# Second layer's stream: six pieces of weights multiplied by Strassen's seven products instead of plainly

## The reference, cut to what matters

```python
    for i in range(DEPTH):
        ...
        x, ctx = trunk_layer(x, ctx, c, c_ctx, p, ang_r, ang_c, need_ctx=(i < DEPTH - 1))
    return x
```

## Time and profile before

| what | value |
|---|---|
| runs | 1561.01, 1561.46, 1563.44 us, median 1561.46 us |
| the profiled execution's own time | 1564.0 us |
| its span (first to last instruction) | 1562.2 us |
| TensorE busy | 1516.4 us, 97% |
| VectorE, ScalarE, GpSimd busy | 681.1, 415.0, 281.9 us |
| mean granted TensorE clock | 0.995 |
| the second a layer begins (its first transposes) | 652.96 us after the start of the span |

### The profile page before, as it was taken

One profiled execution on the slowest core, in us unless ns is written; L12 is line 12 of the kernel. 1 busy time (PEld: TensorE's weight loads), 2 busy tenths in 40 slices (PEclk: granted clock), 3 DMA queues, 4 the chain that ended last, 5 costly groups with the idle time before them and its releaser, 6 DMA issues.

```text
span 1562.2 us, 19171 instructions
## 1 busy us (share of the span) xinstructions
PE 1516.4 (97%) x7888; PEld 1077.2 (69%) x7888; DVE 681.1 (44%) x1460; ACT 415.0 (27%) x814; POOL 281.9 (18%) x314
## 2 busy tenths in 40 slices
PE   6999999999999999999999999999999999999997
PEld 2544544455688885555877888588888758888873
DVE  1233433464633343523344311365687216568721
ACT  1122325232312210121235320134233213423320
POOL 0322210131455441113002102110100011010010
PEclk9999999999999999999999999999999999999999
DMA  8642222300122231322322243423221323332231
GB/s 362 262 175 108 108 108 108 135 27 17 65 81 81 97 123 68 150 108 97 119 108 108 102 156 120 175 102 144 109 110 71 147 115 149 126 112 106 88 128 40
DMA packets 17370, 184.22 MB, mean 118 GB/s; under 512 B 2306, under 2 KB 2818, under 8 KB 4740
## 3 DMA queue, kind: packets, MB, share of 16 engines
q1 hardware_dynamic: 17284, 183.01, 30.7%
HBM read 181.95 MB, written 1.05 MB: 117 GB/s over the span
## 4 chain that ended last, share of the span: by engine, by line
PE 89%; ACT 3%; DVE 3%; issue 2%; DMA 1%; POOL 1%; SPq 0%; POOLq 0%; ACTq 0%; DVEq 0%
PE ps L756 86%; PE ps L811 3%; DVE arena L1749 1%; DVE arena L1755 1%; DMA arena<-in_wf 1%; POOL arena L2362 1%; ACT arena L1333 1%; ACT L1709 0%; ACT L1707 0%; DVE arena L1752 0%; ACT arena L1577 0%; ACT arena L1707 0%; ACT arena L1593 0%; ACT L1595 0%; ACT L1593 0%
## 5 line engine op out<-in xcount | busy, mean ns | idle before, releaser
L756 PE MATMUL ps<-arena 128*128 128x256 f32 (+7 forms) x7396 | 1467.1, 383 | 33.8 <-DMA arena<-in_wf 12.3
L756 PEld LDWEIGHTS ps<-arena 128*128 128x128 f32 (+5 forms) x7396 | 1023.6, 178 | 445.4 <-issue 311.9
L2362 POOL TENSOR_TENSOR arena<-arena 128x256 f32<-128x256 f32 (+6 forms) x254 | 247.3, 994 | 825.8 <-DVE arena L1755 409.3
L1755 DVE SCALAR_TENSOR_TENSOR arena<-arena 128x256 f32<-128x256 f32 (+4 forms) x470 | 231.0, 545 | 143.4 <-ACT arena L1475 38.8
L1333 ACT ACTIVATE arena<-ps 128x512 f32<-128x512 f32 (+2 forms) x280 | 134.9, 505 | 448.3 <-PE ps L756 370.5
L1749 DVE TENSOR_TENSOR arena<-arena 128x512 f32<-128x512 f32 (+14 forms) x190 | 140.4, 761 | 170.9 <-ACT arena L1333 95.8
L1755 DVE SCALAR_TENSOR_TENSOR arena<-arena,ps 128x256 f32<-128x256 f32 (+2 forms) x121 | 54.0, 456 | 207.2 <-PE ps L756 96.9
L1749 DVE TENSOR_TENSOR arena<-ps,arena 128x512 f32<-128x512 f32 (+16 forms) x120 | 48.8, 434 | 106.0 <-PE ps L756 97.3
L811 PEld LDWEIGHTS ps<-arena 128*128 128x128 f32 x488 | 55.7, 141 | 29.4 <-issue 19.5
L811 PE MATMUL ps<-arena 128*128 128x128 f32 x488 | 71.5, 278 | 3.1 <-ACT arena L1611 1.5
L1752 DVE TENSOR_SCALAR arena<-arena 128x256 f32<-128x256 f32 (+9 forms) x181 | 62.8, 382 | 15.7 <-POOL arena L2362 10.8
(11 more groups left out here) (96 smaller groups left out, 294.4 us busy)
## 6 DMA issues: line engine op xcount, KB each, us to landing
arena<-in_wf SPq DMA_DIRECT2D x69, 2048.0 KB, 8.3
arena<-in_wf SPq DMA_DIRECT2D x22, 1024.0 KB, 6.5
arena<-in_wf SPq DMA_DIRECT2D x2, 1152.0 KB, 7.7
arena<-in_xinT SPq DMA_DIRECT2D x2, 1024.0 KB, 15.9
arena<-in_xin SPq DMA_DIRECT2D x4, 512.0 KB, 3.9
arena<-in_rp SPq DMA_DIRECT2D x2, 1024.0 KB, 8.2
arena<-in_consts SPq DMA_DIRECT2D x1, 1410.0 KB, 21.6
arena<-in_pa SPq DMA_DIRECT2D x2, 532.0 KB, 9.4
```

The costliest lines, as they stand in the source:

```text
L756: return e.matmul(o, l, r, start=start, stop=stop, skip_group_check=True)
L1755: return e.scalar_tensor_tensor(out=o, in0=x, scalar=s, in1=y, op0=op0, op1=op1)
L2362: return e.tensor_tensor(o, x, y, op)
```

## The change

Each of six pieces of weights of the second layer (`ag`, `gg`, `su`, `mg0`, `ms0`, `ma1`) is multiplied by seven products of a quarter size. The weights are cut in four quarters (512 input features x 256 output features), the inputs in four (512 features x 128 tokens). A product is eight matmuls of 128 x 128 weights with 128 x 128 inputs (two chunks of output features, four blocks of input features). The four steps of a piece stay where they are in the order and hold products 1 and 2, 6 and 7, 5 and 4, and 3.

- GpSimd makes four sums of weight quarters for each piece (`seven_weights`), two in the step before the piece (`w1`) and two in its first step (`w2`). Three of the four lie in `WW`, one in place of quarter 21 in the ring.
- VectorE makes four differences of the inputs once, ahead of `ag`'s first sum (`HW`).
- Products 6, 5 and 3 go on adding into the bank of product 1, after ScalarE has copied out what stood there; product 4 goes on in the bank of product 7. VectorE makes three sums for each piece (`seven_sums`). In the gated pieces tanh is made by quarters, four instead of four by chunks.
- `HW`, `WW` and a copy `EW` lie in units 4 to 6 of the ring. From `a1ag` to `a1ma1` the ring has four units, and a load waits for the piece two places ahead.

The core of the diff (`seven_result` gives the place of a quarter of the result; `rest_free` is the end of the pieces that lay in units 4 to 6):

```diff
+SEVEN = [[],
+         [("ag", "T"), ("gg", "T"), ("su", "A"), ("mg0", "G"), ("ms0", "G"), ("ma1", "G")]]
...
+    for name, kind in SEVEN[l]:
+        i = [s[:1] for s in steps].index([(name, 0, "T" if kind == "T" else "A")])
+        for k in range(4):
+            steps[i + k] = [(name, x[0], "W" + kind) for x in WINOGRAD[2 * k:2 * k + 2]]
+        steps[i - 1] = steps[i - 1] + [("w1", name, "-")]
+        steps[i] = steps[i] + [("w2", name, "-")]
...
+                if kind[0] != "W":
+                    hold(("dense", l, n, i), b, (dense_act if kind == "A" else dense_dve)(l, n, i))
+                    b = 1 - b
+                elif i == 1:
+                    hold(("dense", l, n, 1), b, dense_dve(l, n, "g12") if kind == "WT" else dense_act(l, n, 3))
+                elif i in (2, 7):
+                    hold(("dense", l, n, i), 1 - b, dense_dve(l, n, 2 if i == 2 else 4))
+                elif i == 3:
+                    b = 1 - b
...
+        short, units = ("a1ag", "a1ma1"), NU
         for name, w in PLAN:
             k = -(-w // UNIT)
-            at = at if at + k <= NU else 0
+            if name == short[0]:
+                rest_free = [done_with[x] for x in tenant[4:] if x]
+                tenant[4:], units = ["rest"] * 3, 4
+            at = at if at + k <= units else 0
...
+            def one_of_seven(l, n, x):
+
+                w = use(f"a{l}{n}", 8)
+                _, s, t, _ = WINOGRAD[[y[0] for y in WINOGRAD].index(x)]
+                if x in (1, 2, 7):
+                    b = bank("dense", l, n, x)
+                else:
+                    b = psum("dense", l, n, 7 if x == 4 else 1)
+                    p.wait_ge(dense_act(l, n, {6: 1, 5: 6, 4: 7, 3: 5}[x]))
...
+                if len(s) == 1:
+                    p.wait_ge(seven_sum(l, n, s))
+                if len(t) == 1:
+                    p.wait_ge(dense_dve(l, "hs", int(t) - 1))
...
+                m = 128 if l else 256
+                for c in range(2):
+                    for k in range(4):
+                        ins = mm(b[:, m * c:m * c + m], W[:, k, 128 * c:128 * c + 128], H[:, k],
+                                 x in (1, 2, 7) and c == k == 0, k == 3)
+                return ins
...
+                if x == 1:
+                    copy(seven_result(l, n, 1, 1), b, scale=scale).then_inc(event(1), 1)
+                elif x == 6:
+                    copy(seven_result(l, n, 2, 1), b).then_inc(event(6), 1)
+                elif x == 7:
...
+                    copy(two_chunks(l, EW), b).then_inc(event(7), 1)
+                    if kind != "WA":
+                        last_th = tanh(1, 1, seven_result(l, n, 1, 1), last_th)
+                elif x == 5:
+                    copy(seven_result(l, n, 2, 2), b).then_inc(event(5), 1)
+                elif kind == "WA":
+                    copy(seven_result(l, n, 1, 2), b, scale=scale).then_inc(event(3), 1)
+                else:
+                    last_th = tanh(2, 1, seven_result(l, n, 2, 1), last_th)
+                    last_th = tanh(1, 2, b, last_th)
...
+                if x in (2, 5, 4):
+                    f, t = {2: (1, 1), 5: (2, 2), 4: (2, 1)}[x]
+                    o = seven_result(l, n, f, t)
+                    b = two_chunks(l, EW if x == 5 else psum("dense", l, n, 7 if x == 4 else 2))
+                    v.wait_ge(dense_done(l, n, x), dense_act(l, n, {2: 1, 5: 5, 4: 6}[x]))
...
+                def make(s, x, y, op, product):
+
+                    if product:
+                        g.wait_ge(*([dense_done(l, SEVEN[l][k - 1][0], product)] if k else rest_free))
+                    tt(w21 if s == "1" else WW[s], x, y, op).then_inc(dn_w.hit(0, 4 * k + "3214".index(s)), 1)
+
+                if first:
+                    g.wait_ge(pieces[name][2])
+                    make("3", w11, w21, ALU.subtract, 7)
+                    g.wait_ge(seven_sum(l, n, "3"))
+                    make("2", w22, WW["3"], ALU.subtract, 6)
+                else:
+                    make("1", w21, w22, ALU.add, None)
+                    g.wait_ge(seven_sum(l, n, "2"))
+                    make("4", w12, WW["2"], ALU.subtract, 3)
```

More of the change, by code:

```diff
@@ L122, in dense_a, with act_events, dve_events @@
             steps += [[("mx", t, "V")] + ada()]
-    return steps + [[("m" + br + str(j), c, "A")] for br, j in EARLY[l] for c in range(4)]
+    steps += [[("m" + br + str(j), c, "A")] for br, j in EARLY[l] for c in range(4)]
+    for name, kind in SEVEN[l]:
[4 more added lines that the diff above has]
+        steps[i] = steps[i] + [("w2", name, "-")]
+    return steps
+def act_events(n, x, kind):
+    if kind[0] != "W":
+        return [(n, x)] if kind in "AT" else []
+    quarters = {7: ["t11"], 4: ["t22"], 3: ["t21"]}.get(x, []) if kind != "WA" else []
+    return ([(n, x)] if x in (1, 6, 7, 5) else []) + [(n, t) for t in quarters] + ([(n, 3)] if x == 3 else [])
+def dve_events(n, x, kind, first):
+    if kind[0] != "W":
+        return [(n, x)] if kind in "TV" else []
+    gated = {7: ["g11"], 4: ["g22"], 3: ["g21", "g12"]}.get(x, []) if kind == "WT" else []
+    return [("hs", i) for i in range(4 if first and x == 1 else 0)] + [(n, t) for t in gated[:1 if x == 4 else 0]] + (
+        [(n, x)] if x in (2, 5, 4) else []) + [(n, t) for t in gated[1 if x == 4 else 0:]]
 def att_pairs(l):
@@ L292, in build_program @@
         BR = r3(X, 4)
+        rest = Mem(arena, 4 * UNIT)
+        HW = {n: rest.take(512) for n in "1234"}
+        WW = {n: r3(rest.take(1024), 4) for n in "234"}
+        EW = rest.take(256)
+        assert rest.at <= NU * UNIT
         SPARE = [[X[:, 512 * c:512 * c + 512] for c in range(4)],
@@ L375, in build_program @@
         DENSE = [dense_a(l) for l in range(2)]
-        FLAT = [[g for step in s for g in step if g[0] != "hx"] for s in DENSE]
+        FLAT = [[g for step in s for g in step if g[0] not in ("hx", "w1", "w2")] for s in DENSE]
         FIRST = [("pf", 0, "A"), ("pf", 1, "A"), ("ps", 0, "V"), ("ps", 1, "V"), ("pf", 2, "A"), ("pf", 3, "A"),
@@ L612, in result, with half_tokens, two_chunks, seven_result @@
             return every_other(x[:, 2 * f - 2:2 * f, :], t)
+        def half_tokens(l, x, t, at=256):
+            return x[:, :, at + 128 * t - 128:at + 128 * t] if l else every_other(x, t)
+        def two_chunks(l, x):
+            return r3(x[:, 0:256], 2) if l else halves(r3(x, 2))
+        def seven_result(l, n, f, t):
+            if n == "gqk":
+                return half_tokens(l, GQ if f == 1 else GK, t)
+            x, at = {"ag": (AG, 256), "gg": (GG, 256), "su": (SG, 256), "mg0": (AG, 0), "ms0": (GG, 0), "ma1": (SG, 0)}[n]
+            return half_tokens(l, x[:, 2 * f - 2:2 * f, :], t, at)
         def gates(f, t):
```

108 lines of the change are left out of this document (98 added, 10 removed).

## The result

The changed kernel takes 1574.19 us, median of four runs (1572.65 to 1577.31), against 1562.38 us for the kernel before on the same chip (four runs): ratio 1.0083, 95% interval 1.0065 to 1.0101. It is slower by 12 to 13 us, where the forecast was 6.3 us faster, with 1559.3 us as the upper end of the range. The profiled execution took 1574.03 us, its span is 1572.2 us.

A forecast was written before the change was run, and what follows sets the result against it. TensorE, busy 97% of the span, was taken as the bound. Terms -7.9 + 1.1 + 0.2 + 0.3 = -6.3 us took the median from 1561.5 to 1555.2 us; the 8-in-10 range was 1552.5 to 1559.3.

The forecast's parts named there:

- Spacing of the records: TensorE, six pieces: 128-column records 0.1117 us apart, a piece 12.51 us instead of 13.82, gain 7.9 us in all.
- The estimate from the two spacings of the Trainium skill: TensorE: 128-column spacing 0.83 of that for 256 columns, a piece 20.1 us, the kernel some 38 us slower.
- For small lateness elsewhere: VectorE's sum ahead of a predicated copy, VectorE slower beside GpSimd's sums: 0.3 us, between 0 and 1.
- These waits are satisfied when TensorE comes to them.: Bank hand-overs to products 3 to 7: each has 1.79 us of cover and mostly more, so they cost nothing.
- VectorE's room: VectorE and ScalarE have room in the stretches for the added work; it costs only where something stands right behind it.
- `su`'s second product: It takes the bank of `gg`'s product 3 with 0.1 us slack: stall 0 to 0.4 us, taken as 0.2.
- `ms0`, product 6: GpSimd's levels 4 and 5 queue behind two sums, delaying ScalarE's copy: TensorE stalls 1.1 us (0.2 to 2.1).
- Ring, loads: Loads issued two pieces ahead land 8.3 us later, in time: cost nothing, unless a load took 4 us longer.
- Behind the stream: Merge, `ou` and b layers follow the last products at the same distances; the 0.55 us gap at 984.05 stays.
- Rival 2: GpSimd's queue becomes the bound at `ms0` or `mg0`: 1556.2 us, or up to 10 us more on TensorE, 1564; chance 5%, slower.

The follow-up runs named there:

- the kernel with sums cut for `ma1`: Changed kernel with only `ma1`'s four GpSimd sums cut in four instructions, the other 20 whole; 1565.31 us, ratio 1.0029 to the kernel before.
- the kernel with 16-column sums: Changed kernel with each GpSimd weight sum making only 16 of its 1024 columns, for its time alone; 1554.14 us, ratio 0.9954 to the kernel before.
- sums in four: Changed kernel with each GpSimd sum of 128x1024 made as four instructions of 128x256; 1557.42 us, ratio 0.9975 to the kernel before.
- plain products: Products of the kernel before, with the ring of four units and GpSimd sums nobody uses; ratio to before 1.0000 with whole sums, 1.0004 with 16 columns.

## Why the prediction was wrong, step by step

- **Spacing of the records.** Right. In the changed kernel 32 of these records take 3.57 us (781.43 to 785.00), 0.1116 each, against 0.1117 in the forecast; the 48 of `gg` in the kernel with sums cut for `ma1` take 5.46, 0.1138 each. The stream of the kernel with 16-column sums gained 7.8 us, forecast 7.9. The estimate from the two spacings of the Trainium skill (TensorE: Matmul & The Clock Gate, Back-to-back issue gap), 38 us slower, is denied.
- **"For small lateness elsewhere ... I take 0.3 us, between 0 and 1": the step that failed.** It held "VectorE slower beside the sums". Measured, 19.0 us: 13.6 of waits, 13.0 of them for VectorE, and 3.8 of lower clock, 1.6 not split further. The rows for it were in front of me: a sum of 3.32 us with VectorE busy 13.16 of 13.20, and 2.35 with it busy 1.27 of 4.80. I read them as two engines that slow each other, and charged GpSimd alone. The single operations would have shown it: of VectorE's eight there, the four additions of 128x1024 (both inputs in SBUF) take 1.22 us for the first, which started ahead of GpSimd's sum, and 3.25 to 3.37 for the next three, while the four of 128x512 that read PSUM take 0.67 each. Each engine stands while the other works, which is also why a sum takes 3.32 us there.
- **"These waits are satisfied when TensorE comes to them."** Wrong for those that VectorE ends. The hand-over was costed as 0.38 + 0.42 us behind the product, with nothing ahead in VectorE's queue. In the changed kernel 4.6 us (`gg`) and 7.7 us (`ma1`) of operations beside sums were ahead.
- **VectorE's room.** "VectorE and ScalarE have room for that": it is busy 34.85 of 55 and 35.94 of 64 us in the two stretches, so there was room; a share does not show a queue held for 2.5 us at a time.
- **`su`'s second product**, forecast 0 to 0.4 us: TensorE stood 1.0 us ahead of the first and 1.5 us ahead of the second. The gates of `gg` read SBUF alone, and one took 1.95 us; a level's product queued between them took 2.50.
- **`ms0`, product 6**, forecast 1.1 (0.2 to 2.1): in the changed kernel no wait there; TensorE had by then stood 8.6 us at earlier places. With sums in four it came, 1.7 us, along the chain that was described, and it went when the two sums were moved. The mechanism was right, the size 0.6 low.
- **Ring, loads**: nothing, as forecast (ratio 1.0004).
- **Behind the stream**: the gap behind the merge grew from 0.55 to 0.89 us, in the kernel with 16-column sums too (0.90), but not with plain products (0.55). It ends with VectorE's last gate, which starts 0.61 us after the first of the transposes there instead of 0.26. Why was not found.
- **Rival 2** had GpSimd's queue as the way to a slower kernel, at 5%. It was not the cause; with eight instructions for a sum it becomes one. The clock was in no term and no rival.

Two views that the first and second points rest on, of TensorE in the changed kernel and of VectorE in the kernel before:

```profile
781.43 3.74 PE L833 MATMUL ps<-arena 128*128 128x128 f32 x32
785.00 0.60 PE L888 MATMUL ps<-arena 128*128 128x128 f32 x4
...
402.39 11.09 DVE L1749 TENSOR_TENSOR arena<-arena 128x1024 f32<-128x1024 f32 x4
413.40 2.47 DVE L1755 SCALAR_TENSOR_TENSOR arena<-arena,ps 128x512 f32<-128x512 f32 x4
```

## What to carry to other kernels

Before putting work on GpSimd, list what VectorE does beside it: an operation that reads only SBUF may wait for a whole GpSimd instruction, whatever its own size (additions, `scalar_tensor_tensor` and `tensor_scalar` did here, the reciprocal did not). Cut GpSimd's long instructions so that one holds VectorE for about as long as VectorE's own operations take (0.7 us here), but not further, since each cut costs GpSimd time and its own queue then becomes late. And when a bank or buffer is handed on by another engine than before, look at what stands ahead in that engine's queue, not at its busy share.

## What the runs showed of the hardware

- An addition of one column (128x1, SBUF) takes 0.16 us, and 2.30 us beside a GpSimd addition of 128x1024.
- Beside the same kind of sum, VectorE operations that read PSUM keep their time (421 ns for 128x256), and so does a reciprocal of two columns in SBUF (0.17 us).
- GpSimd's sum of 1024 columns takes 2.35 us with VectorE out of its way and 2.52 in the mean; 256 columns take 0.72 and 128 columns 0.40, so by these the same sum would take 2.9 and 3.2 us in pieces. GpSimd's busy time between 640 and 990 us grew by 0.6 us a sum with four pieces and by 1.1 with eight.
- TensorE's granted clock was 0.68 in the 5 us behind a wait of 2.28 us (level 1.2 GHz for part of it). In the same kernel run again, and in the one with sums cut for `ma1` alone, nearly the same wait, 2.29 us, was followed by 1.00. What decides it the runs don't show (windows of these two, columns as above):

```profile
759.70:764.70 5.00, 4.95 (x44) 4.95 (x45) 2.95 (x7) 0.72 (x3) 0.11 (x1) 1.00 0.16 69
...
760.40:765.40 5.00, 4.94 (x44) 4.94 (x45) 2.96 (x8) 0.72 (x3) 0.11 (x1) 1.00 0.19 82
```
